# Turning softmax weights: TensorE transposes replaced by 32x32 squares on VectorE and a trip through DRAM

## The chip, the cores and the metric

The kernel runs on one core of a Trainium2 chip. The metric is the device time in microseconds of one execution. Engine names: TensorE is PE in the profile, VectorE is DVE, ScalarE is ACT, GpSimd is POOL, and SyncE (SP) issues most DMAs.

## The reference, cut to what matters

The layer projects x (2048 x 1024) into many columns, runs four branches (stick-breaking attention, pooling, a gated recurrence, attention over a memory), and merges them. The change touches the last one:

```python
def memory_cross_attention(q, mem, w_mem_kv):
    kv = mem @ w_mem_kv
    k = kv[..., :XA_WIDTH].reshape(b, m, XA_HEADS, XA_HEAD_DIM)      # m = 256, 4 heads of 128
    v = kv[..., XA_WIDTH:].reshape(b, m, XA_HEADS, XA_HEAD_DIM)
    scores = jnp.einsum('bshd,bmhd->bhsm', qh, k) / math.sqrt(XA_HEAD_DIM)
    p = jax.nn.softmax(scores, axis=-1)
    out = jnp.einsum('bhsm,bmhd->bshd', p.astype(v.dtype), v)
```

## The kernel before

The sequence is worked in two halves of 1024 rows (T), each in two chunks of 512 (C; c = 0, 1). The projections are 72 "pairs" of 128-column tiles, 36 in each half, each done as 14 "pieces" of six matmuls (a product in three passes, fp32r high and low parts). All engines walk the same list of pieces in an order written out by hand. Work of the branches is hung in between as hooks: on TensorE a hook with number i comes in front of piece i, on the other engines behind their work for piece i. A pair is fed with weights like this: SyncE loads RAW (one half at piece 1, one at piece 12), GpSimd makes sums of them (SR) and, with VectorE, the low parts (WLS, WL), ScalarE the high parts (WHS, WH). ScalarE copies finished banks J out and VectorE adds the others to them (the sums for pieces 5, 9, 11 and 13).

The memory branch takes the pairs XA0 to XA0+3 (queries of head h and its gate), and the first pair of merge 3. In pair XA0+h the weights of head h-1 are finished, and after it the scores of head h are made:

- memory_scores (PE, after the pair): 24 matmuls into BR, c=0 in the banks ZZ, c=1 in AO. Before c=1 it waits for y_f of head h-1, because the values of head h-1 lie in AO.
- memory_max (DVE hook 1), memory_weights (ACT, eight exponentials with row sums into PR), memory_norm (DVE, PR times 1/sum).
- memory_turned: PE turns PR (rows on partitions) into memory positions on partitions, 16 transposes of 128x128 into BR in front of piece 9; ACT hook 8 copies the high part PTH out of PSUM, DVE hook 8 makes the rest PTL = BR - PTH.
- memory_values (PE in front of piece 12): 12 matmuls of VM with PTH and PTL into AO.
- memory_output (DVE hook 12): Y = AO * Y, and y_f rises.
- memory_queries: ACT and DVE hooks 9 and 10 split the queries of head h into XQH and XQL.

There are four heads and two halves, so this runs eight times: six times in a pair XA0+1 to XA0+3, twice in the merge pair, which has no queries and no scores behind it.

Of the kernel before, what the change touches and what calls it, by code (L numbers as in the profile page):

```python
# [39 lines left out]

MEM_TILES = 2 * HEADS

C_ID, C_NEVER, C_CNT = 0, P, 2 * P
# [130 lines left out]
def build(nc, xt, xrow, memt, w8, w4, wgate, wpool, prm, cst, ln_g, ln_b, out):  # L174
    with ExitStack() as ctx:
# [88 lines left out]
        XQR = at("XQR", R + 48, [T])  # L264
        AG = [at(f"AG{i}", R + 52 + 4 * i, [T]) for i in range(2)]
        KM = [at(f"KM{i}", R + 68.25 + i, [MEM], F32R) for i in range(2)]
        VM = [at(f"VM{i}", R + k, [MEM // P, P], F32R) for i, k in enumerate((70.25, 28))]
# [24 lines left out]
        pk_v = nc.dram_tensor("pk_v", (HEADS, P, SEQ // P, 2, P), F32).ap()  # L292
        pk_y = nc.dram_tensor("pk_y", (2, P, T), F32).ap()
        pk_m = nc.dram_tensor("pk_m", (FT, P, T), F32).ap()
        km_keep = nc.dram_tensor("km_keep", (2, P, HEADS * MEM), F32).ap()
# [49 lines left out]
        sc_done, pt_hi, mx_done, ex_done = sem("sc_done"), sem("pt_hi"), sem("mx_done"), sem("ex_done")  # L345
        nm_done, tr_done, pt_done, xo_done = sem("nm_done"), sem("tr_done"), sem("pt_done"), sem("xo_done")

# [49 lines left out]
        def unit(half, u):  # L397

            return raw_block(*PLAIN[u]) if u in PLAIN else sum_of(half, u), XBH[u][:], XBL[u][:]

        def row_number(t, part):
# [25 lines left out]
        def _(sp):  # L427
# [167 lines left out]
            def load_memory_values(half, h):  # L595
# [5 lines left out]
                for i in range(2):  # L601
                    sp.dma_start(VM[i][:].rearrange("p m d -> p (m d)").bitcast(F32),
                                 vm_keep[i, :, h * MEM:(h + 1) * MEM]).then_inc(vm_back, 16)

            def merge(half, n):
                g0 = half * PAIRS + (M0, M1, M2, M3)[n]
# [10 lines left out]
                if n:  # L617
                    def first_weights():
                        if n == 1:
                            sp.wait_ge(mix_done, HEADS * (half + 1))  # L620
                        elif n == 2:
                            sp.wait_ge(xc_f, HEADS * (half + 1))
                        else:
                            sp.wait_ge(sc_done, 4 * HEADS * (half + 1))
                        load_b(half, n, 0)
                    hooks = {8: first_weights}
                    if n == 2:
                        hooks[5] = lambda: order_gates(half, HEADS - 1)
                    pair(g0, hooks)
# [79 lines left out]
            for half in range(HALVES):  # L709
# [15 lines left out]
                for n, first in enumerate((POOL0, LRU0, XA0)):  # L725
                    for h in range(HEADS):
                        hooks = {}
                        if n == 1:
                            hooks = {5: lambda: (load_gate_weights(half, h), h and order_gates(half, h - 1))}
                        if n == 2 and not h:  # L730
                            hooks = {5: lambda: load_memory_values(half, h)}
                        elif n == 2:
                            hooks = {0: lambda: load_memory_keys(half, h), 13: lambda: load_memory_values(half, h)}
                        pair(g0 + first + h, hooks)
                    merge(half, n + 1)
# [35 lines left out]
        def _(pe):  # L771
# [215 lines left out]
            def memory_scores(half, h):  # L987
                hh = half * HEADS + h
                pe.wait_ge(km_back, 32 * (hh + 1))
                pe.wait_ge(xq_lo, hh + 1)  # L990
                if h == 0:
                    pe.wait_ge(mu_done, f_count(half, 2))
                wait_if(pe, pt_done, 4 * hh)
                for c in range(NC):
                    if c:
                        wait_if(pe, y_f, y_count(half, 3, h))
                    for t in range(C // P):
                        q = slice(c * C + t * P, c * C + (t + 1) * P)
                        to = BR[c][t // 2][:, (t % 2) * MEM:(t % 2 + 1) * MEM]
                        mm = pass3(to, (XQH[:, q], XQL[:, q]), (KM[0][:], KM[1][:]), True)  # L1000
                        if t % 2:
                            mm.then_inc(sc_done, 1)

            def memory_turned(half, h):
                hh = half * HEADS + h
                for c in range(NC):
                    pe.wait_ge(nm_done, 4 * (NC * hh + c + 1))
                    for m in range(MEM // P):
                        for t in range(C // P):
                            mm = nc.tensor.transpose(BR[c][m][:, t * P:(t + 1) * P], PR[c][:, t, m * P:(m + 1) * P],  # L1010
                                                     IDENT[:])
                        mm.then_inc(tr_done, 1)

            def memory_values(half, h):
                hh = half * HEADS + h
                pe.wait_ge(pt_done, 4 * (hh + 1))
                pe.wait_ge(vm_back, 32 * (hh + 1))
                for c in range(NC):
                    for m in range(MEM // P):
                        mm = pass3(BR[1][c][:], (VM[0][:, m, :], VM[1][:, m, :]), (PTH[c][:, m, :], PTL[c][:, m, :]), m == 0)  # L1020
                    mm.then_inc(xo_done, 1)

            for half in range(HALVES):
# [17 lines left out]
                for h in range(HEADS):  # L1041
                    pair(g0 + XA0 + h, {9: lambda: memory_turned(half, h - 1),
                                        12: lambda: memory_values(half, h - 1)} if h else {})
                    memory_scores(half, h)
                merge(half, 3, {9: lambda: memory_turned(half, HEADS - 1), 12: lambda: memory_values(half, HEADS - 1)})

# [51 lines left out]
        def _(act):  # L1099
# [182 lines left out]
            def keys_of(h):  # L1282
                act.wait_ge(mk_done, h + 1)
                nc.scalar.copy(KMA[0][:, h, :], KBANK[h][:, 0:MEM]).then_inc(mk_hi, 1)

# [238 lines left out]
            def memory_weights(half, h):  # L1524
                hh = half * HEADS + h
                wait_if(act, tr_done, 4 * hh)
                for c in range(NC):
                    act.wait_ge(mx_done, 2 * (NC * hh + c) + 2)
                    for t in range(C // P):
# [5 lines left out]
            def memory_turned(half, h):  # L1535
                hh = half * HEADS + h
                wait_if(act, xo_done, NC * hh)
                for c in range(NC):
                    for m in range(MEM // P):
                        act.wait_ge(tr_done, 2 * (NC * hh + c) + m + 1)  # L1540
                        if h == 0 and c:
                            wait_kept(act, half, 2, 6)
                        nc.scalar.copy(PTH[c][:, m, :], BR[c][m][:]).then_inc(pt_hi, 1)

# [3 lines left out]
            for half in range(HALVES):  # L1548
# [42 lines left out]
                for h in range(HEADS):  # L1591
                    hooks = {9: lambda: memory_queries(half, h)}
                    if h:
                        hooks[1] = lambda: memory_weights(half, h - 1)
                        hooks[5] = lambda: memory_silu(half, h - 1)
                        hooks[8] = lambda: memory_turned(half, h - 1)
                    pair(g0 + XA0 + h, hooks)
                merge(half, 3, {1: lambda: memory_weights(half, HEADS - 1), 5: lambda: memory_silu(half, HEADS - 1),
                                8: lambda: memory_turned(half, HEADS - 1)})

# [47 lines left out]
        def _(dve):  # L1649
# [124 lines left out]
            def keys_rest(h):  # L1774
                dve.wait_ge(mk_hi, h + 1)
                V_.tensor_tensor(KMA[1][:, h, :], KBANK[h][:, 0:MEM], KMA[0][:, h, :].bitcast(F32),
                                 ALU.subtract).then_inc(mk_free, 1)

# [293 lines left out]
            def memory_norm(half, h):  # L2072
                hh = half * HEADS + h
                for c in range(NC):
# [3 lines left out]
                    for t in range(C // P):  # L2078
                        V_.tensor_scalar(PR[c][:, t, :], PR[c][:, t, :], SM[:, m + 12 + t:m + 13 + t], None,
                                         ALU.mult).then_inc(nm_done, 1)  # L2080

            def memory_queries(half, h):
# [4 lines left out]
            def memory_turned(half, h):  # L2087
                hh = half * HEADS + h
                wait_if(dve, xo_done, NC * hh)
                for c in range(NC):  # L2090
                    for m in range(MEM // P):
                        dve.wait_ge(pt_hi, 2 * (NC * hh + c) + m + 1)
                        if h == 0 and c:
                            wait_kept(dve, half, 2, 7)
                        V_.tensor_tensor(PTL[c][:, m, :], BR[c][m][:], PTH[c][:, m, :].bitcast(F32), ALU.subtract
                                         ).then_inc(pt_done, 1)

            def memory_output(half, h):
                hh = half * HEADS + h
                for c in range(NC):  # L2100
                    dve.wait_ge(xo_done, NC * hh + c + 1)
                    dve.wait_ge(sil, (half * NB + 3) * KB + h + 1)
                    y = Y[h][:, c * C:(c + 1) * C]
                    V_.tensor_tensor(y, BR[1][c][:], y, ALU.mult).then_inc(y_f, 1)

# [39 lines left out]
            for half in range(HALVES):  # L2145
# [58 lines left out]
                def hooks_of(h):  # L2204

                    return {1: lambda: memory_max(half, h), 5: lambda: memory_norm(half, h),
                            8: lambda: memory_turned(half, h), 11: lambda: silu(half, 3, h, AG[h % 2][:]),
                            12: lambda: memory_output(half, h)}

# [296 lines left out]
```

## Time and profile before

| what | value |
|---|---|
| median of 3 runs | 2308.84 us (2308.07 to 2308.89) |
| span of the profiled execution, first to last instruction | 2306.2 us |
| what is listed of the profiled execution's own time | the span alone |
| PE busy | 2293.5 us (99%) |
| PEld, DVE, ACT, POOL busy | 82%, 61%, 46%, 53% |
| granted TensorE clock | 0.999 of full speed |
| DMA | mean 122 GB/s |

The busy shares are over the whole span. Matmuls are pipelined, so a busy PE row says only that PE has no gap. A timeline row has the start, the length, the engine and the line, and for several instructions of a kind in a row their number.

### The profile page before, as it was taken

How to read it: one execution, taken by the hardware profiler on the slowest of the kernel's cores; microseconds unless marked ns; L12 is line 12 of the kernel's file. 1: busy time of each engine (PE TensorE's matmuls, PEld its weight loads, DVE VectorE, ACT ScalarE, POOL GpSimd, SP SyncE). 2: the span in 40 equal slices, each digit the busy share in tenths (PEclk: the TensorE clock that was granted, in tenths of full speed). 3: DMA queues.
4: the chain of work that ended last, by engine and by line, in shares of the span. 5: the costliest groups of instructions: out<-in, count | busy, mean ns of one | idle time of the engine just before them, and what ended most of it. 6: DMA issues, size and time to landing. Idle time of an engine off the chain costs nothing.

```text
span 2306.2 us, 30158 instructions
## 1 busy us (share of the span) xinstructions
PE 2293.5 (99%) x10952; PEld 1901.2 (82%) x10952; DVE 1405.1 (61%) x1658; ACT 1060.3 (46%) x1643; POOL 1219.1 (53%) x847
## 2 busy tenths in 40 slices
PE   9999999999999999999999999999999999999998
PEld 6888888888878888888888888888888778888887
DVE  7556552763476465468877777723744595465476
ACT  5555542442484255332576676632342683355220
POOL 1666653864456354435476566645763555345341
PEclk9999999999999999999999999999999999999999
DMA  6544422124343312374344544332233334312442
GB/s 233 188 157 157 146 73 96 55 83 137 103 112 124 132 51 77 102 275 144 105 161 139 165 154 132 116 99 71 57 126 130 85 110 141 103 55 86 143 168 82
DMA packets 102898, 281.06 MB, mean 122 GB/s; under 512 B 9952, under 2 KB 31584, under 8 KB 101728
## 3 DMA queue, kind: packets, MB, share of 16 engines
q1 hardware_dynamic: 101024, 273.90, 36.2%
q10 hardware_dynamic: 1728, 5.24, 0.7%
q8 instruction: 88, 1.44, 0.3%
q14 instruction: 58, 0.48, 0.1%
HBM read 207.80 MB, written 62.91 MB: 117 GB/s over the span
## 4 chain that ended last, share of the span: by engine, by line
PE 99%; DMA 1%; DVE 0%; issue 0%; DVEq 0%
PE J L775 21%; PE J L777 21%; PE J L776 21%; PE AO L947 8%; PE ZZ L947 8%; PE AO L777 3%; PE AO L776 3%; PE AO L775 3%; PE ZZ L777 2%; PE ZZ L776 2%; PE ZZ L775 2%; PE AO L901 1%; PE JX L901 1%; PE ZZ L982 1%; PE ZZ L870 1%; PE AO L860 0%
## 5 line engine op out<-in xcount | busy, mean ns | idle before, releaser
L2290 POOL TENSOR_TENSOR WLS<-SR,WHS 128x512 fp32r<-128x512 f32 x264 | 407.8, 1563 | 118.8 <-ACT WHS L1118 110.7
L775 PE MATMUL J<-XBH,WHS 128*128 128x512 f32 x1152 | 453.1, 393 | 0.0
L777 PE MATMUL J<-XBH,WLS 128*128 128x512 f32 x1152 | 449.3, 390 | 0.0
L776 PE MATMUL J<-XBL,WHS 128*128 128x512 f32 x1152 | 448.9, 390 | 0.0
L775 PE MATMUL J<-XBH,WH 128*128 128x512 f32 x864 | 340.0, 394 | 0.2
L777 PE MATMUL J<-XBH,WL 128*128 128x512 f32 x864 | 337.0, 390 | 0.0
L776 PE MATMUL J<-XBL,WH 128*128 128x512 f32 x864 | 336.8, 390 | 0.0
L777 PEld LDWEIGHTS J<-XBH,WLS 128*128 128x128 f32 x1152 | 216.2, 188 | 46.0
L776 PEld LDWEIGHTS J<-XBL,WHS 128*128 128x128 f32 x1152 | 216.5, 188 | 43.4 <-issue 0.2
L775 PEld LDWEIGHTS J<-XBH,WHS 128*128 128x128 f32 x1152 | 216.4, 188 | 43.3 <-DVE XBL L1671 0.2
L1704 DVE TENSOR_TENSOR ST<-J,ST 128x512 f32<-128x512 f32 x160 | 109.6, 686 | 228.9 <-PE J L777 178.6
L2282 POOL TENSOR_TENSOR SR<-RAW 128x512 f32<-128x512 f32 x71 | 105.3, 1483 | 269.0 <-DMA RAW<-w 236.8
L2339 POOL TENSOR_TENSOR REST<-REST,SHARE 128x512 f32<-128x512 f32 (+3 forms) x160 | 165.5, 1037 | 118.2 <-DVE REST L1859 114.8
L2356 POOL TENSOR_TENSOR BL<-BRAW,BH 128x512 fp32r<-128x512 f32 x64 | 89.3, 1400 | 222.8 <-ACT BH L1386 222.6
L775 PEld LDWEIGHTS J<-XBH,WH 128*128 128x128 f32 x864 | 162.3, 188 | 39.3 <-issue 7.3
L777 PEld LDWEIGHTS J<-XBH,WL 128*128 128x128 f32 x864 | 162.2, 188 | 34.7
L776 PEld LDWEIGHTS J<-XBL,WH 128*128 128x128 f32 x864 | 162.3, 188 | 31.8 <-issue 0.2
L1118 ACT CAST WHS<-SR 128x1024 fp32r<-128x1024 f32 x144 | 151.5, 1052 | 77.0 <-POOL SR L2282 75.9
L2282 POOL TENSOR_TENSOR SR<-SR,RAW 128x512 f32<-128x512 f32 x71 | 102.6, 1445 | 113.9 <-PE J L777 111.7
L1200 ACT COPY ST<-J 128x512 f32<-128x512 f32 x160 | 94.0, 589 | 139.7 <-PE J L777 136.7
L1859 DVE TENSOR_TENSOR_SCAN REST<-KEEP,REST,ZZ 128x513 f32<-128x513 f32 x96 | 122.8, 1279 | 25.5 <-ACT SHARE L1328 24.4
L2282 POOL TENSOR_TENSOR SR<-RAW,SR 128x512 f32<-128x512 f32 x71 | 101.0, 1422 | 68.2 <-PE J L777 67.5
(302 smaller groups left out, 4748.9 us busy)
## 6 DMA issues: line engine op xcount, KB each, us to landing
RAW<-w SPq DMA_DIRECT2D x144, 512.0 KB, 3.7
pk_m<-MB SPq DMA_DIRECT2D x56, 512.0 KB, 5.0
MB<-pk_m SPq DMA_DIRECT2D x48, 512.0 KB, 4.1
KC<-pk_k SPq DMA_DIRECT2D x40, 512.0 KB, 5.3
VC<-pk_v SPq DMA_DIRECT2D x40, 512.0 KB, 4.4
BRAW<-w SPq DMA_DIRECT2D x64, 256.0 KB, 5.2
XRAW<-xt SPq DMA_DIRECT2D x8, 1024.0 KB, 12.4
pk_v<-STL SPq DMA_DIRECT2D x16, 512.0 KB, 5.1
```

The lines of the kernel that those rows point to most:

```text
L775: nc.tensor.matmul(to, wh, xh, start=first, stop=True, skip_group_check=True)
L776: nc.tensor.matmul(to, wh, xl, start=False, stop=True, skip_group_check=True)
L777: return nc.tensor.matmul(to, wl, xh, start=False, stop=True, skip_group_check=True)
L947: mm = nc.tensor.matmul(BR[p][c][:], w[p][:, k, :], y[k][:, c * C:(c + 1) * C], start=(k == 0 and m == 0), stop=(k == KB - 1 and m == 2))
L1118: nc.scalar.copy(WHS[:, k, :], SR[:, k, :]).then_inc(w_hi, 1)
L1200: nc.scalar.copy(dest(g)[p][:, c * C:(c + 1) * C], J[(g + bank) % 2][:]).then_inc(cp_done, 1)
L1704: V_.tensor_tensor(d, bank[:], d, ALU.add).then_inc(ad_done, 1)
L1859: V_.tensor_tensor_scan(REST[:, j, 0:n + 1], KEEP[:, gs % 2, 0:n + 1], ZB[gs % 2][:, 0:1].broadcast_to([P, n + 1]), 1.0 if diag else REST[ ...
L2282: G_.tensor_tensor(SR[:, 4 * j:4 * j + 4], a, b, op).then_inc(s_raw, 1)
L2290: low = G_.tensor_tensor(WLS[:, k, :], SR[:, k, :], WHS[:, k, :].bitcast(F32), ALU.subtract)
L2339: G_.tensor_tensor(w, w, SHARE[gs % 2][:, 0:n], ALU.mult).then_inc(w_done, 1)
L2356: G_.tensor_tensor(BL[f % 2][:], BRAW[f % 2][:], BH[f % 2][:].bitcast(F32), ALU.subtract).then_inc(b_lo, 1)
```

## The change

The 16 transposes on TensorE go. In their place:

1. The memory keys are stored with their 256 columns in another order, so that the columns of the scores come in four groups (by_group).
2. After the norm of each c VectorE turns PR (128x1024) in one instruction: every 32x32 square is turned in itself, into PB.
3. SyncE (move_blocks, hook 3) writes PB to DRAM, one DMA of 512 KB for each c, and when that has landed reads it back into PR with four DMAs of 128 KB, each to 32 partitions in runs of 1 KB. Now memory positions lie on the partitions.
4. ScalarE copies PTH from PR and VectorE makes PTL from PR and PTH, one 128x1024 instruction for each c instead of two of 128x512 out of PSUM.
5. The hooks move: ACT's exponentials from 1 to 0 and its copies from 8 to 10; DVE's norm from 5 to 3, its silu from 11 to 5, its rests from 8 to 9, its output from 12 to 13; PE's values from 12 to 13, with a wait for each c.

```diff
+        PB = [at(f"PB{c}", R + 4 + 4 * c, [C // P * MEM]) for c in range(NC)]
+        PB_LAST = [at(f"PBL{c}", R + k, [C // P * MEM]) for c, k in enumerate((32, 52))]
+            def move_blocks(half, h):
+                hh = half * HEADS + h
+                for c in range(NC):
+                    sp.wait_ge(pb_made, NC * hh + c + 1)
+                    sp.dma_start(pk_t[c], blocks_of(h)[c][:]).then_inc(pb_kept[c], 16)
+                for c in range(NC):
+                    sp.wait_ge(pb_kept[c], 16 * (hh + 1))
+                    rows = pk_t[c].rearrange("(i r) (g x) -> g r i x", i=GROUPS, g=GROUPS)
+                    for g in range(GROUPS):
+                        to = PR[c][SQUARE * g:SQUARE * (g + 1)].rearrange("p t m -> p (t m)")
+                        sp.dma_start(to.rearrange("p (i x) -> p i x", i=GROUPS), rows[g]).then_inc(pt_in[c], 16)
...
+                    if n == 3:
+                        hooks[3] = lambda: move_blocks(half, HEADS - 1)
...
-                            hooks = {0: lambda: load_memory_keys(half, h), 13: lambda: load_memory_values(half, h)}
+                            hooks = {0: lambda: load_memory_keys(half, h), 3: lambda: move_blocks(half, h - 1),
+                                     13: lambda: load_memory_values(half, h)}
...
-                wait_if(pe, pt_done, 4 * hh)
+                wait_if(pe, ex_done, 4 * NC * hh)
...
-            def memory_turned(half, h):
-                hh = half * HEADS + h
-                for c in range(NC):
-                    pe.wait_ge(nm_done, 4 * (NC * hh + c + 1))
-                    for m in range(MEM // P):
-                        for t in range(C // P):
-                            mm = nc.tensor.transpose(BR[c][m][:, t * P:(t + 1) * P], PR[c][:, t, m * P:(m + 1) * P],
-                                                     IDENT[:])
-                        mm.then_inc(tr_done, 1)
...
-                pe.wait_ge(pt_done, 4 * (hh + 1))
                 pe.wait_ge(vm_back, 32 * (hh + 1))
                 for c in range(NC):
+                    pe.wait_ge(pt_done, NC * hh + c + 1)
...
-                    pair(g0 + XA0 + h, {9: lambda: memory_turned(half, h - 1),
-                                        12: lambda: memory_values(half, h - 1)} if h else {})
+                    pair(g0 + XA0 + h, {13: lambda: memory_values(half, h - 1)} if h else {})
                     memory_scores(half, h)
-                merge(half, 3, {9: lambda: memory_turned(half, HEADS - 1), 12: lambda: memory_values(half, HEADS - 1)})
+                merge(half, 3, {13: lambda: memory_values(half, HEADS - 1)})
...
-                nc.scalar.copy(KMA[0][:, h, :], KBANK[h][:, 0:MEM]).then_inc(mk_hi, 1)
+                nc.scalar.copy(by_group(KMA[0][:, h, :]), by_tile(KBANK[h][:, 0:MEM])).then_inc(mk_hi, 1)
...
-                wait_if(act, tr_done, 4 * hh)
                 for c in range(NC):
+                    wait_if(act, pt_done, NC * (hh - 1) + c + 1)
...
-                    for m in range(MEM // P):
-                        act.wait_ge(tr_done, 2 * (NC * hh + c) + m + 1)
-                        if h == 0 and c:
-                            wait_kept(act, half, 2, 6)
-                        nc.scalar.copy(PTH[c][:, m, :], BR[c][m][:]).then_inc(pt_hi, 1)
+                    act.wait_ge(pt_in[c], 16 * GROUPS * (hh + 1))
+                    if h == 0 and c:
+                        wait_kept(act, half, 2, 6)
+                    nc.scalar.copy(as_product(PTH[c]), as_moved(c)).then_inc(pt_hi, 1)
...
-                        hooks[1] = lambda: memory_weights(half, h - 1)
+                        hooks[0] = lambda: memory_weights(half, h - 1)
                         hooks[5] = lambda: memory_silu(half, h - 1)
-                        hooks[8] = lambda: memory_turned(half, h - 1)
+                        hooks[10] = lambda: memory_turned(half, h - 1)
...
+                    dve.wait_ge(nm_done, 4 * (NC * hh + c + 1))
+                    wait_if(dve, pb_kept[c], 16 * hh)
+                    V_.transpose(blocks_of(h)[c].rearrange("p (g t x) -> p t g x", g=GROUPS, t=C // P), PR[c][:]
+                                 ).then_inc(pb_made, 1)
...
-                        V_.tensor_tensor(PTL[c][:, m, :], BR[c][m][:], PTH[c][:, m, :].bitcast(F32), ALU.subtract
-                                         ).then_inc(pt_done, 1)
+                    V_.tensor_tensor(as_product(PTL[c]), as_moved(c), as_product(PTH[c]).bitcast(F32), ALU.subtract
+                                     ).then_inc(pt_done, 1)
...
-                    y = Y[h][:, c * C:(c + 1) * C]
-                    V_.tensor_tensor(y, BR[1][c][:], y, ALU.mult).then_inc(y_f, 1)
+                    y = Y[h][:, c * C:(c + 1) * C].rearrange("p (t i q) -> p i t q", i=GROUPS, q=SQUARE)
+                    made = BR[1][c].rearrange("p (i t q) -> p i t q", i=GROUPS, q=SQUARE)
+                    V_.tensor_tensor(y, made, y, ALU.mult).then_inc(y_f, 1)
...
-                    return {1: lambda: memory_max(half, h), 5: lambda: memory_norm(half, h),
-                            8: lambda: memory_turned(half, h), 11: lambda: silu(half, 3, h, AG[h % 2][:]),
-                            12: lambda: memory_output(half, h)}
+                    return {1: lambda: memory_max(half, h), 3: lambda: memory_norm(half, h),
+                            5: lambda: silu(half, 3, h, AG[h % 2][:]), 9: lambda: memory_turned(half, h),
+                            13: lambda: memory_output(half, h)}
```

## Rows read from the trace of the kernel before

**Rows 1.** The page: the chain that ended last, shares of the span by engine.
```profile
PE 99%; DMA 1%; DVE 0%; issue 0%; DVEq 0%
```

**Rows 2.** Critical chain, 868 to 895: start us, us, what.
```profile
880.55 0.88 PE ZZ L1010 x8
881.43 0.87 PE AO L1010 x8
```

**Rows 3.** Timeline of PE: start us, us, line, operation, out<-in.
```profile
868.12 0.40 PE L775 MATMUL J<-XBH,WH 128*128 128x512 f32 x1
...
883.29 0.39 PE L777 MATMUL J<-XBH,WLS 128*128 128x512 f32 x1
...
891.48 0.39 PE L777 MATMUL J<-XBH,WL 128*128 128x512 f32 x1
891.71 0.28 PE L775 MATMUL ZZ<-KM,XQH 128*128 128x256 f32 x1
...
893.14 0.28 PE L775 MATMUL AO<-KM,XQH 128*128 128x256 f32 x1
...
894.58 0.40 PE L775 MATMUL J<-XBH,WH 128*128 128x512 f32 x1
```

**Rows 4.** Timeline of DVE, same pair.
```profile
878.58 2.19 DVE L2079 TENSOR_SCALAR PR<-PR,SM 128x256 f32<-128x256 f32 x4
880.69 1.21 DVE L1722 TENSOR_TENSOR WL<-RAW,WH 128x1024 fp32r<-128x1024 f32 x1
...
884.22 0.68 DVE L1704 TENSOR_TENSOR XQR<-J,XQR 128x512 f32<-128x512 f32 x1
...
889.96 1.29 DVE L2104 TENSOR_TENSOR Y<-AO,Y 128x512 f32<-128x512 f32 x2
891.90 0.69 DVE L1704 TENSOR_TENSOR AG<-J,AG 128x512 f32<-128x512 f32 x1 [0.66 <-PE J L777]
```

**Rows 5.** Timeline of ACT, same pair and the one behind it.
```profile
871.60 0.48 ACT L1531 ACTIVATE PR<-ZZ,SM 128x256 f32<-128x256 f32 x1
...
875.21 0.64 ACT L1200 COPY AG<-J 128x512 f32<-128x512 f32 x1
...
884.93 1.06 ACT L1522 ACTIVATE XQH<-XQR 128x1024 fp32r<-128x1024 f32 x1 [0.85 <-DVE XQR L1704]
...
925.29 3.89 ACT L1402 CAST YH<-Y 128x1024 fp32r<-128x1024 f32 x4
```

**Rows 6.** Timeline of POOL, same pair.
```profile
883.82 1.29 POOL L2282 TENSOR_TENSOR SR<-RAW,SR 128x512 f32<-128x512 f32 x1 [3.21 <-PE J L777]
885.25 3.52 POOL L2290 TENSOR_TENSOR WLS<-SR,WHS 128x512 fp32r<-128x512 f32 x2
888.74 2.28 POOL L2282 TENSOR_TENSOR SR<-RAW,RAW 128x512 f32<-128x512 f32 x1
```

**Rows 7.** Timeline of DVE and POOL, 298 to 310.
```profile
301.98 2.32 DVE L1722 TENSOR_TENSOR WL<-RAW,WH 128x1024 fp32r<-128x1024 f32 x1
...
303.18 2.29 POOL L2282 TENSOR_TENSOR SR<-RAW,RAW 128x512 f32<-128x512 f32 x1
...
308.14 0.17 DVE L1832 TENSOR_SCALAR SM<-SM 128x4 f32<-128x4 f32 x1
...
308.19 1.29 POOL L2356 TENSOR_TENSOR BL<-BRAW,BH 128x512 fp32r<-128x512 f32 x1 [2.72 <-ACT BH L1386]
308.35 1.15 DVE L1831 TENSOR_TENSOR SM<-SM 128x4 f32<-128x4 f32 x1
```

**Rows 8.** DMA issues: out<-in, KB each, median us from issue to landing.
```profile
pk_q<-ST SPq DMA_DIRECT2D x8, 512.0 KB, 2.7
...
LI<-XC SPq DMA_DIRECT2D x8, 256.0 KB, 4.6
KM<-km_keep SPq DMA_DIRECT2D x16, 128.0 KB, 2.7
```

**Rows 9.** Timeline of SP's queue, same pair.
```profile
868.31 0.79 SPq L593 DMA_DIRECT2D KM<-km_keep  x2
```

More of the change, by code:

```diff
@@ L41 @@
 MEM_TILES = 2 * HEADS
+SQUARE = 32
+GROUPS = P // SQUARE
 C_ID, C_NEVER, C_CNT = 0, P, 2 * P
@@ L293, in build @@
         pk_y = nc.dram_tensor("pk_y", (2, P, T), F32).ap()
+        pk_t = nc.dram_tensor("pk_t", (NC, P, C // P * MEM), F32).ap()
         pk_m = nc.dram_tensor("pk_m", (FT, P, T), F32).ap()
@@ L345, in build @@
         sc_done, pt_hi, mx_done, ex_done = sem("sc_done"), sem("pt_hi"), sem("mx_done"), sem("ex_done")
-        nm_done, tr_done, pt_done, xo_done = sem("nm_done"), sem("tr_done"), sem("pt_done"), sem("xo_done")
+        nm_done, pt_done, xo_done = sem("nm_done"), sem("pt_done"), sem("xo_done")
+        pb_made, pb_kept, pt_in = sem("pb_made"), [sem(f"pb_kept{c}") for c in range(NC)], [sem(f"pt_in{c}") for c in range(NC)]
         wo_hi = sem("wo_hi")
@@ L399, in unit, with blocks_of, by_group, by_tile @@
             return raw_block(*PLAIN[u]) if u in PLAIN else sum_of(half, u), XBH[u][:], XBL[u][:]
+        def blocks_of(h):
+            return PB_LAST if h + 1 == HEADS else PB
+        def by_group(keys):
+            return keys.rearrange("p (g b r) -> p b g r", g=GROUPS, b=MEM // P)
+        def by_tile(keys):
+            return keys.rearrange("p (b g r) -> p b g r", g=GROUPS, b=MEM // P)
+        def as_moved(c):
+            return PR[c][:].rearrange("p t m -> p (t m)").rearrange("p (n b q) -> p n b q", b=MEM // P, q=SQUARE)
+        def as_product(tile):
+            return tile[:].rearrange("p b (n q) -> p n b q", q=SQUARE)
         def row_number(t, part):
@@ L1593, in _ @@
                     if h:
-                        hooks[1] = lambda: memory_weights(half, h - 1)
+                        hooks[0] = lambda: memory_weights(half, h - 1)
                         hooks[5] = lambda: memory_silu(half, h - 1)
-                        hooks[8] = lambda: memory_turned(half, h - 1)
+                        hooks[10] = lambda: memory_turned(half, h - 1)
                     pair(g0 + XA0 + h, hooks)
-                merge(half, 3, {1: lambda: memory_weights(half, HEADS - 1), 5: lambda: memory_silu(half, HEADS - 1),
-                                8: lambda: memory_turned(half, HEADS - 1)})
+                merge(half, 3, {0: lambda: memory_weights(half, HEADS - 1), 5: lambda: memory_silu(half, HEADS - 1),
+                                10: lambda: memory_turned(half, HEADS - 1)})
                 def split_rows(t, ks):
@@ L1775, in keys_rest @@
                 dve.wait_ge(mk_hi, h + 1)
-                V_.tensor_tensor(KMA[1][:, h, :], KBANK[h][:, 0:MEM], KMA[0][:, h, :].bitcast(F32),
-                                 ALU.subtract).then_inc(mk_free, 1)
+                V_.tensor_tensor(by_group(KMA[1][:, h, :]), by_tile(KBANK[h][:, 0:MEM]),
+                                 by_group(KMA[0][:, h, :].bitcast(F32)), ALU.subtract).then_inc(mk_free, 1)
             def first_sums(second):
@@ L2090, in memory_turned @@
                 for c in range(NC):
[L2091 to L2094, printed above, removed]
-                        V_.tensor_tensor(PTL[c][:, m, :], BR[c][m][:], PTH[c][:, m, :].bitcast(F32), ALU.subtract
-                                         ).then_inc(pt_done, 1)
+                    dve.wait_ge(pt_hi, NC * hh + c + 1)
+                    if h == 0 and c:
+                        wait_kept(dve, half, 2, 7)
+                    V_.tensor_tensor(as_product(PTL[c]), as_moved(c), as_product(PTH[c]).bitcast(F32), ALU.subtract
+                                     ).then_inc(pt_done, 1)
             def memory_output(half, h):
```

## The prediction

> **What bounds the kernel now.** I read the page's chain of waits first: 99% of it is TensorE [rows 1]. No other engine is waited for, so a microsecond comes off the time only if TensorE gets less work, and is lost as soon as TensorE waits. Next I read the timelines of one memory pair on each engine. I count t from the pair's first matmul at 868.12; the next pair starts at 894.58, so a pair takes 26.46 us, without a gap [rows 3]. The reader should see in it: a piece is six matmuls of 0.227 us, 1.36 us; the 16 transposes stand before piece 9; the 24 score matmuls come at the end, the ZZ half (c=0) first and the AO half (c=1) 1.43 us later [rows 3]. In that stretch VectorE, ScalarE and GpSimd idle for much of it, but in short gaps, and what matters is where each step of the softmax lands.
>
> **What is removed.** The 16 transposes of a head: 0.88 + 0.87 us [rows 2]. Eight heads (four in each half), so 8 x 1.75 = -14.0 us, all on the path. The ScalarE and VectorE passes out of PSUM are replaced by passes of the same element count.
>
> **What is free.** The regrouping of the key columns at the start and the permuted views of Y touch the same elements; I cost them at 0 (VectorE's and ScalarE's 1024 elements stay 1024). The scores' wait moves from the rests to the exponentials, long past in both. Dropping the PSUM banks earlier gives nothing, because no one waits for them.
>
> **The new chain, step by step** (pairs XA0+1 to XA0+3, h-1 = 0, 1, 2).
> Maxima: if VectorE is kept by the outputs at the end of the pair before (below), they end at t = 1.3 (c=0) and 2.5 (c=1). Exponentials, at hook 0 now: eight from 871.60 to 875.21, 0.45 each [rows 5], so 1.35 to 3.2 and to 5.0. The piece copy behind them on ScalarE comes at 5.0 instead of 3.0, and TensorE needs it at piece 6, t = 8.2: covered by 3 us.
> Norm: 1.15 us for c=0; for c=1 2.19 us, one of its four having stood while GpSimd ran [rows 4].
> VectorE transposes of 128x1024: the trace has none. Bounds: 0.68 us for 512 elements doubled in rate at the low end, 2.19 us at the high end; nearest is a 1024-element pass, 1.21 us [rows 4]. I take 1.2. Blocks made at t = 5.9 (c=0) and 9.4 (c=1). VectorE's sum after piece 5 slips by 1 us, covered until the next use of that bank.
> SyncE: a 512 KB write lands in 2.7 us (the pk_q row), a 128 KB load in 2.7 us, and an issue takes 0.4 us [rows 8, 9]. SyncE issues c=0's four reads only behind c=1's write (it waits for c=1's blocks first): 9.85 to 11.4, landed by 14.3. The write for c=1 lands at 13, its reads by 17.5. Upper bound for the last of four queued loads is the 4.6 us of LI<-XC [rows 8], which gives 16.0 and 19. What is queued behind these waits on SyncE is the load of RAW at piece 12, which waits for GpSimd's fourth sum, t = 22.9 today [rows 6], and in the merge pair the loads of BRAW, which are split only after that pair: both covered.
> ScalarE, hook 10: it comes behind the cast of the queries, which waits for the sum after piece 9. The sum starts 0.42 us after piece 13's last matmul (891.48, 891.90) and the cast 0.71 after the sum [rows 3 to 5]. Without the transposes piece 9's last matmul starts at 883.29 - 1.75, t = 13.4, so sum 13.85, cast 14.6, and the two copies (0.96 apart, 3.89 us for four [rows 5]) end at 16.6 and 17.6, if c=0 has landed by 15.6.
> VectorE: the rest PTL. Before, one operand lay in PSUM. Now both lie in SBUF, as in WL<-RAW,WH, and that is where I think the cost is.
>
> **Two operands in SBUF beside GpSimd.** A four-element VectorE operation took 1.15 us (its like before it 0.17), from 308.35 to 309.50, while GpSimd ran from 308.19 to 309.48; WL took 2.32 us instead of 1.21, and GpSimd's next one 2.29 instead of 1.29 [rows 4, 7]. So the two take turns: each waits until the other's instruction is over, and whoever waits goes next. The Trainium skill states such a rule (SBUF — State Buffer, "SBUF: two separate sides"): VectorE with two SBUF inputs and GpSimd hold one port pair exclusively. The trace agrees (the 1.15 us).
> Today GpSimd runs SR at 883.82 and two WLS from 885.25 [rows 6]. They follow piece 9, so they move 1.75 earlier: WLS at t = 15.4 to 16.65 and 16.65 to 17.9, then the fourth SR. PTL for c=0 asks at 16.65, when the second WLS starts. I take GpSimd as first (any delay in front of ScalarE's copy gives that, and VectorE's silu, now at hook 5, and its WL, one GpSimd turn apart from t = 10.5 to 13.9, leave the sum after piece 9 no slack): PTL c=0 runs 17.8 to 18.95, SR 18.9 to 20.05, PTL c=1 20.05 to 21.2.
> TensorE reaches the values at 13 x 1.36 = 17.7. It waits to 18.95 (1.25), runs six matmuls to 20.3, waits to 21.2 (0.9). Six times (three pairs in each half): 6 x 2.15 = +12.9 us.
> Behind PTL on VectorE stand the rest of the queries (1.2 us, to 22.4; the scores start at 23.9) and the sum for piece 11, and behind ScalarE's copies its copy for piece 11, which TensorE needs in the next pair: all covered. So is the reload of VM, which waits for the last values and is wanted a pair later.
> In the merge pair there is no query cast; PTL c=0 is ready in time and c=1, behind its load and one GpSimd turn, at 20.0 against 19.05: 2 x 1.0 = +2.0 us.
>
> **The output's new place.** It moves from hook 12 to 13, behind the sum for piece 13, while the AO half of the scores overwrites its bank. The sum starts at 891.90 and takes 0.69, the two outputs take 1.29 [rows 4]: 893.88. The AO scores start at 893.14 [rows 3]: a wait of 0.7 us, six times (after the merge pair no scores follow): +4.2 us. This one I regard as certain; before, the outputs ran at 889.96, inside piece 13.
>
> **Sum.** -14.0 + 12.9 + 2.0 + 4.2 = +5.1 us. The profiled execution spans 2306.2; the median is 2308.84, 2.6 us more for what lies around the span. I add the difference to the median: 2313.9, called 2314.
>
> **Rivals.**
> A, VectorE wins the turn at 16.65: PTL c=0 ends at 17.8, GpSimd's WLS until 18.9, PTL c=1 ends at 20.05. TensorE waits 0.1 and 0.9: 6 x 1.0 = 6.0. Sum -14.0 + 6.0 + 2.0 + 4.2 = -1.8: 2307.0. The two requests are within 0.1 us of each other; for it speaks that ScalarE's copy is reckoned without delay, against it that every delay lies on this side.
> B, the other sign: the rests meet no turn of GpSimd. PTL ends at 17.8 and 18.9, TensorE waits 0.1, and nothing in the merge pair: -14.0 + 0.6 + 4.2 = -9.2: 2299.6. It decides if the second WLS of GpSimd falls outside 16.6 to 17.8 or if this form doesn't take turns; rows 7 speak against the latter.
> C, the loads are late: each read goes to 32 partitions in 1 KB runs, a shape that no row has, and c=1's write runs beside c=0's reads. If c=0 lands at 17 and c=1 at 20.5, PTL c=1 ends at 22.8 (copy 1.05, rest 1.2) instead of 21.2, and in the merge pair at 22.8 instead of 20.0: 6 x 1.6 + 2 x 2.8 = 15 more: 2329; half of that lateness gives 2321. It costs from a landing of c=1 at about 18.9 on. 
>
> **Chances.** Forecast 0.43, A 0.22, B 0.15, C 0.20. 0.2% is 4.6 us, about what a measurement of this kernel can tell from no change. The forecast lies just beyond it: of its 0.43 I put 0.28 on slower and 0.15 on same. A gives same 0.18, faster 0.04. B is faster, C slower. Together faster 0.19, same 0.33, slower 0.48. The forecast's own range is 2310 to 2318 (3 us on each side: half a turn of GpSimd, 0.6 us, in six pairs). The range for 8 in 10 leaves out most of B and the far half of C: 2302 to 2325.
>
> **What the profile after would show.** TensorE's pair from first matmul to first matmul: 27.6 us if I am right (26.46 - 1.75 + 2.15 + 0.7), 26.4 in A, 25.5 in B. TensorE idle before AO<-PTH, put down to PTL, twice in a pair, and idle before AO<-KM put down to VectorE's Y. PTL at about 2.3 us instead of 1.2. The transpose near 1.2 us. In C ScalarE's copy PTH idles for the DMA. Wrong would make it above all a different order of requests near t = 16.6, and a load that lands after 15.6.

## The result, and the profile after

The changed kernel takes 2313.66 us (median of 10 runs, 2313.03 to 2314.68) against 2308.57 us before. The ratio of the two is 1.0023, with a 95% interval of 1.0015 to 1.0032: 5.1 us slower. One of the ten executions of the kernel before took 4679.57 us, for a reason that nothing here shows; without it its median is 2308.56. The profiled execution spans 2311.7 us, 5.5 more than before.

The page of the changed kernel: busy time and instructions, then the chain that ended last by engine.

```profile
span 2311.7 us, 29983 instructions
...
PE 2285.3 (99%) x10824; PEld 1886.3 (82%) x10824; DVE 1444.2 (62%) x1658; ACT 1059.8 (46%) x1627; POOL 1226.4 (53%) x847
...
PE 95%; DVE 2%; DMA 1%; issue 1%; ACT 1%; SPq 0%; DVEq 0%; ACTq 0%
```

TensorE has less work (2285.3 us busy instead of 2293.5), yet it is now 95% of the chain where it was 99% [rows 1]: 4% more of the chain runs through VectorE, ScalarE and issue.

The timeline of TensorE in the pair XA0+3 of the first half. Count t from 869.50, as the prediction counts it from 868.12.

```profile
869.50 0.40 PE L817 MATMUL J<-XBH,WH 128*128 128x512 f32 x1
...
886.98 0.39 PE L819 MATMUL J<-XBH,WL 128*128 128x512 f32 x1
888.61 0.47 PE L817 MATMUL AO<-PTH,VM 128*128 128x512 f32 x1 [1.25 <-DVE PTL L2128]
...
889.85 0.39 PE L819 MATMUL AO<-PTH,VM 128*128 128x512 f32 x1
890.74 0.50 PE L817 MATMUL AO<-PTH,VM 128*128 128x512 f32 x1 [0.50 <-DVE PTL L2128]
...
894.95 0.28 PE L819 MATMUL ZZ<-KM,XQL 128*128 128x256 f32 x1
895.78 0.39 PE L817 MATMUL AO<-KM,XQH 128*128 128x256 f32 x1 [0.55 <-DVE Y L2138]
...
897.32 0.40 PE L817 MATMUL J<-XBH,WH 128*128 128x512 f32 x1
```

The pair takes 27.82 us (869.50 to 897.32) where it took 26.46 [rows 3]. Piece 12's last matmul is at 886.98; the values should follow 0.23 later and come 1.63 later, on PTL. Their second half waits again (889.85 to 890.74), and the AO half of the scores waits for VectorE's Y (894.95 to 895.78, where the next such matmul follows 0.12 later). The three releasers in the brackets are the three that the prediction named.

VectorE in the same pair:

```profile
874.20 1.25 DVE L2113 STREAM_TRANSPOSE PB<-PR 128x1024 f32<-128x1024 f32 x1
...
875.54 1.95 DVE L2109 TENSOR_SCALAR PR<-PR,SM 128x256 f32<-128x256 f32 x4
877.52 1.25 DVE L2113 STREAM_TRANSPOSE PB<-PR 128x1024 f32<-128x1024 f32 x1
...
886.17 4.52 DVE L2128 TENSOR_TENSOR PTL<-PR,PTH 128x1024 fp32r<-128x1024 f32 x2 [2.14 <-ACT PTH L1573]
...
894.44 1.28 DVE L2138 TENSOR_TENSOR Y<-AO,Y 128x512 f32<-128x512 f32 x2
895.64 1.73 DVE L1765 TENSOR_TENSOR WL<-RAW,WH 128x512 fp32r<-128x512 f32 x1
```

The transposes of 128x1024 take 1.25 us. The second norm is 1.95 us with GpSimd in the way [rows 4]. The two rests PTL take 4.52 us together. ScalarE and GpSimd in the same pair:

```profile
885.04 1.03 ACT L1573 CAST PTH<-PR 128x1024 fp32r<-128x1024 f32 x1
886.43 1.05 ACT L1573 CAST PTH<-PR 128x1024 fp32r<-128x1024 f32 x1 [0.36 <-DMA PR<-pk_t]
```

```profile
884.84 2.54 POOL L2324 TENSOR_TENSOR WLS<-SR,WHS 128x512 fp32r<-128x512 f32 x2
887.35 2.26 POOL L2316 TENSOR_TENSOR SR<-RAW,RAW 128x512 f32<-128x512 f32 x1
```

ScalarE's copy for c=0 is done at 886.07 and VectorE asks at 886.17, t = 16.67. GpSimd's first WLS began at 884.84, and the second one starts at 886.10 (its row shows the two as one). VectorE is 0.07 us behind it and waits the whole of it. Then it runs, GpSimd's SR (887.35, 2.26 us instead of 1.29) waits for it, and VectorE's second rest waits for SR in turn.

The pair XA0+1 of the first half, from 815.03, shows the other order. VectorE, then GpSimd:

```profile
831.64 3.45 DVE L2128 TENSOR_TENSOR PTL<-PR,PTH 128x1024 fp32r<-128x1024 f32 x2 [2.07 <-ACT PTH L1573]
835.01 2.30 DVE L2118 SCALAR_TENSOR_TENSOR XQL<-XQR,XQH 128x1024 fp32r<-128x1024 f32 x1
```

```profile
830.39 3.61 POOL L2324 TENSOR_TENSOR WLS<-SR,WHS 128x512 fp32r<-128x512 f32 x2
833.97 2.26 POOL L2316 TENSOR_TENSOR SR<-RAW,RAW 128x512 f32<-128x512 f32 x1
```

Here VectorE asks at 831.64, t = 16.61, 6 ns ahead of GpSimd's second WLS, and goes first: 3.45 us for both rests instead of 4.52, and the pair takes 26.68 us (815.03 to 841.71) instead of 27.8. It is the only one of six in this execution.

All 16 rests, with their shortest, median and longest time in ns, and what TensorE waited for them:

```profile
L2128 DVE TENSOR_TENSOR PTL<-PR,PTH x16: 1226/2296/2322, 831.6 to 2110.8; 128x1024 fp32r<-128x1024 f32 x16
...
  PE AO L817: 10.4, 13
  PEld AO L817: 7.5, 8
```

The new loads, with the median time from issue to landing:

```profile
PR<-pk_t SPq DMA_DIRECT2D x64, 128.0 KB, 3.4
...
```

### The profile page after: what moved, and what is told of

The parts are those of the page before. It is cut to its first block, busy times and chain, and to the rows that moved or that the text cites. A ratio compares the mean times of both kernels' runs of the same rounds, so it can differ in the third digit from the quotient of the medians.

```text
span 2311.7 us, 29983 instructions
## 1 busy us (share of the span) xinstructions
PE 2285.3 (99%) x10824; PEld 1886.3 (82%) x10824; DVE 1444.2 (62%) x1658; ACT 1059.8 (46%) x1627; POOL 1226.4 (53%) x847
## 4 chain that ended last, share of the span: by engine, by line
PE 95%; DVE 2%; DMA 1%; issue 1%; ACT 1%; SPq 0%; DVEq 0%; ACTq 0%
PE J L817 20%; PE J L819 20%; PE J L818 20%; PE AO L989 8%; PE ZZ L989 8%; PE AO L817 2%; PE AO L819 2%; PE AO L818 2%; PE ZZ L819 2%; PE ZZ L818 2%; PE ZZ L817 2%; PE AO L943 1%; PE JX L943 1%; DVE PTL L2128 1%; PE ZZ L1024 1%
```

## The experiments

Every kernel was timed against the kernel before on its own chip. "Difference" is from that kernel's median (2308.46 us in the first four, 2308.18 in the last three); the changed kernel has +5.1.

### The output back at 12

```diff
-                            13: lambda: memory_output(half, h)}
+                            12: lambda: memory_output(half, h)}
```

> The changed kernel with one hook put back: VectorE's outputs of the memory branch at 12 again, ahead of the sum for piece 13. Theory of the output's place: the AO scores wait 0.7 us for Y in six pairs, so that wait goes and the time falls by six times 0.7, 4.3 us, to about 2309.4, and a pair takes 27.1 us instead of 27.8. Rival, the sum for piece 13 is what the next pair needs and only the place of the wait moves: no change, 2313.7.

Measured: 2307.57 us, ratio 0.9995 (0.9986 to 1.0004), a difference of -0.9, so 6.0 us better than the change. TensorE's timeline in the same pair:

```profile
869.11 0.40 PE L817 MATMUL J<-XBH,WH 128*128 128x512 f32 x1
...
888.25 0.47 PE L817 MATMUL AO<-PTH,VM 128*128 128x512 f32 x1 [1.26 <-DVE PTL L2128]
...
890.37 0.50 PE L817 MATMUL AO<-PTH,VM 128*128 128x512 f32 x1 [0.50 <-DVE PTL L2128]
...
896.14 0.40 PE L817 MATMUL J<-XBH,WH 128*128 128x512 f32 x1
```

The pair takes 27.03 us, 0.8 less, and the waits for PTL stand as they were. Five pairs gain 0.8 each, 4.0 us. Not expected were two things. The maxima of the next pair start 1.3 us earlier: the outputs are made sooner, and the WL between them and the maxima takes 0.69 us, where in the changed kernel it meets GpSimd's WLS and takes 1.73 (895.64). So the moved data land sooner, and the wait in the two merge pairs goes, 2.2 us (21.8 us for each up to the next pair, instead of 22.9). There ScalarE's two copies now stand close together, t = 13.85 from that pair's start at 896.14, where they waited 1.09 and 1.26 us for their loads in the changed kernel:

```profile
909.99 2.22 ACT L1573 CAST PTH<-PR 128x1024 fp32r<-128x1024 f32 x2
```

Against that, the pair XA0+1 of the first half lost its turn (26.99 us instead of 26.68). VectorE, then GpSimd:

```profile
831.75 4.60 DVE L2128 TENSOR_TENSOR PTL<-PR,PTH 128x1024 fp32r<-128x1024 f32 x2 [2.07 <-ACT PTH L1573]
```

```profile
830.49 2.55 POOL L2324 TENSOR_TENSOR WLS<-SR,WHS 128x512 fp32r<-128x512 f32 x2
```

VectorE asks at t = 16.61 as it did in this pair of the changed kernel, but this time 4 ns behind the start of GpSimd's second WLS, and waits it out. 4.0 + 2.2 - 0.3 = 5.9.

### GpSimd held until the rests are made

```diff
                 elif i == 9:
                     sum_raw(g + 1, 2)
...
+                    if XA0 < l <= M3:
+                        pool.wait_ge(pt_done, NC * (half * HEADS + l - XA0))
                     if not quiet(g + 1) and not apart:
                         rest_of_sums(g + 1, False)
```

> The changed kernel with GpSimd held: in the eight pairs in which memory weights are turned, GpSimd waits for both rests PTL before its two WLS for the next pair. Theory of the turns: PTL takes 1.2 us instead of 2.3, TensorE waits about 0.1 us for c=0 and up to 0.4 us for c=1 (its load lands near t = 17), instead of 2.3 us in all: 14.4 us of waiting for the rests in eight pairs becomes at most 4, so the time falls by 10 to 14 us, to 2300 to 2303.5. Rival, the moved data are late and PTL is only the messenger: the waits stay where they are, within 1 us in a pair, and the time stays at 2308 or above. Second rival, GpSimd's weights are then late for the next pair: TensorE waits before piece 2 there, and the time stays or rises.

Measured: 2301.68 us, ratio 0.9972 (0.9961 to 0.9983), a difference of -6.8, 11.9 us better than the change. The rests and TensorE's waits for them, all eight pairs:

```profile
L2128 DVE TENSOR_TENSOR PTL<-PR,PTH x16: 1218/1226/1228, 832.0 to 2098.8; 128x1024 fp32r<-128x1024 f32 x16
...
  PE AO L817: 0.9, 5
```

VectorE and GpSimd in the pair XA0+3 of the first half:

```profile
883.90 2.36 DVE L2128 TENSOR_TENSOR PTL<-PR,PTH 128x1024 fp32r<-128x1024 f32 x2 [2.13 <-ACT PTH L1573]
```

```profile
886.34 3.46 POOL L2324 TENSOR_TENSOR WLS<-SR,WHS 128x512 fp32r<-128x512 f32 x2 [3.89 <-DVE PTL L2128]
```

The two rests take 2.36 us instead of 4.52, and TensorE's waits for them 0.9 us in all instead of 17.9. Late data (the first rival) are not what cost the time in these six pairs. That is seen best in the pair XA0+2 of the first half, ScalarE, then VectorE:

```profile
858.29 1.05 ACT L1573 CAST PTH<-PR 128x1024 fp32r<-128x1024 f32 x1 [0.44 <-DMA PR<-pk_t]
```

```profile
859.38 1.23 DVE L2128 TENSOR_TENSOR PTL<-PR,PTH 128x1024 fp32r<-128x1024 f32 x1 [0.20 <-ACT PTH L1573]
```

Here the load holds ScalarE's copy for c=1 until t = 17.01 (the pair starts at 841.28), as late as the 16.93 of the pair XA0+3 above, yet the rest takes 1.23 us and no matmul waits for it. The edit does also make the loads land sooner, by up to 1.5 us for c=1 (pair XA0+3): GpSimd's later WLS no longer meet VectorE's WL in front of the maxima (0.68 us instead of 1.73), and the maxima of the pairs behind another memory pair start 1.1 us sooner. In the merge pairs, where c=1's load did hold up its rest, that helps to end the wait: 21.8 us up to the next pair instead of 22.9. GpSimd's WLS start at t = 19.1 (886.34 less the pair's start at 867.23) instead of 15.3, and no one in the next pair waits for them (the second rival).

### ScalarE's copy for c=0 ahead of the queries

```diff
-                        hooks[10] = lambda: memory_turned(half, h - 1)
+                        hooks[9] = lambda: (memory_turned(half, h - 1, (0,)), memory_queries(half, h))
+                        hooks[10] = lambda: memory_turned(half, h - 1, (1,))
```

> The changed kernel with ScalarE's copy of PTH for c=0 ahead of the cast of the queries, in the pairs with both. Theory of the turns: PTL c=0 then asks near t = 16.1, before GpSimd's first WLS ends, and gets the turn that it lost by 0.08 us, so TensorE waits only for c=1, about 1 us: the five pairs that took 27.8 take about 26.6, so the time falls by about 6 us, to 2307.5. If the queries were what matters (they come 1 us later), the scores in ZZ would wait and nothing would be gained: 2313 or more. Rival, the loads for c=0 land only near t = 16: gain below 2 us.

Measured: 2305.83 us, ratio 0.9990 (0.9981 to 0.9999), a difference of -2.6, 7.7 us better than the change. ScalarE and VectorE in the pair XA0+3 of the first half, which starts at 867.19:

```profile
882.13 1.05 ACT L1573 CAST PTH<-PR 128x1024 fp32r<-128x1024 f32 x1 [1.00 <-DMA PR<-pk_t]
...
884.38 1.05 ACT L1573 CAST PTH<-PR 128x1024 fp32r<-128x1024 f32 x1 [0.24 <-DMA PR<-pk_t]
```

```profile
883.28 1.64 DVE L2129 TENSOR_TENSOR PTL<-PR,PTH 128x1024 fp32r<-128x1024 f32 x1 [1.55 <-ACT PTH L1573]
885.46 1.69 DVE L2129 TENSOR_TENSOR PTL<-PR,PTH 128x1024 fp32r<-128x1024 f32 x1 [0.54 <-ACT PTH L1573]
```

No engine does less here; VectorE only asks at t = 16.09, while GpSimd's first WLS still runs, and the rests fall to 1.64 and 1.69 us. This pair takes 26.55 us (foretold 26.6), as three others do. The first memory pair of each half takes 25.47: there TensorE waits for no rest at all, which had not been foretold and accounts for the 1.7 us beyond the expected gain. ScalarE's first copy waited for its load until t = 14.94, which tells when c=0 lands: 14.9, and c=1 at t = 17.2 (884.38), against 14.3 and 17.5 foretold. The prediction's estimate from the Trainium skill's rate for 32 partitions (SBUF — State Buffer, "Door 1: The DMA port swizzle") was near 15 and near 18; for c=0 the run agrees with it more closely (14.94), for c=1 it does not (17.2). The rate itself is not measured by this, since SyncE issues the eight loads over 4.36 us, one in 0.5 us or so.

### GpSimd held and the output at 12

Both edits together.

> Both of the first two edits. If the two waits are separate, the gains add: 10 to 14 and 4.3, to 2295.5 to 2299, faster than the kernel before. If one hides the other: no better than the better of the two alone.

Measured: 2296.91 us, ratio 0.9950 (0.9937 to 0.9962), a difference of -11.6. The output's place gives 4.8 us on top of the held GpSimd (-6.8 to -11.6), which is 0.8 in six pairs: the two waits are separate. The merge pair's, which the second edit also cured alone, is already gone by the first; in this execution 0.1 and 0.4 us of it come back. Pairs take 25.1 us.

### The kernel before with only its last hooks moved

```diff
-                                        12: lambda: memory_values(half, h - 1)} if h else {})
+                                        13: lambda: memory_values(half, h - 1)} if h else {})
...
-                            12: lambda: memory_output(half, h)}
+                            13: lambda: memory_output(half, h)}
```

> The kernel before with only the hooks of the values and of the output moved, both from 12 to 13; transposes, PSUM banks and all else as they were. Theory of the output's place: TensorE waits before the AO scores for Y in six pairs and nowhere else, 0.7 to 0.8 us each as after the change: 4.2 to 4.9 us more, 2312.7 to 2313.4. Rival, the wait comes only with the new chain: no change, 2308.5.

Measured: 2312.92 us, ratio 1.0020 (1.0011 to 1.0029), a difference of +4.7. TensorE's timeline in the pair XA0+3:

```profile
870.08 0.40 PE L775 MATMUL J<-XBH,WH 128*128 128x512 f32 x1
...
894.98 0.28 PE L777 MATMUL ZZ<-KM,XQL 128*128 128x256 f32 x1
895.81 0.39 PE L775 MATMUL AO<-KM,XQH 128*128 128x256 f32 x1 [0.55 <-DVE Y L2104]
...
897.35 0.40 PE L775 MATMUL J<-XBH,WH 128*128 128x512 f32 x1
```

The place of the output costs its 4.7 us in the kernel before as well, with transposes and all: six pairs, 0.8 each (27.27 us instead of 26.46). No matmul waits in front of the values, so it is not their move that costs.

### A quarter of the transposes

```diff
-                        for t in range(C // P):
+                        for t in (C // P - 1,):
```

> The kernel before with 4 of a head's 16 transposes, one for each bank, so three quarters of the turned weights are left out of the computation. Each transpose costs TensorE 0.109 us (1.75 for 16), so 12 x 8 of them give 10.5 us: 2298.0. If the transposes lay partly beside other work, less: 2301 or more.

Measured: 2301.05 us, ratio 0.9967 (0.9954 to 0.9979), a difference of -7.1; the span falls by 8.1 (2298.1). That is 2.4 to 3.4 us short of what was expected, and the median lies where the expectation's rival has it (2301 or more, if the transposes lay partly beside other work), so the time alone does not decide between the two. The trace does. TensorE around the four that are left:

```profile
878.27 0.38 PE L1010 MATMUL ZZ<-IDENT,PR 128*128 128x128 f32 x2
878.70 0.44 PE L1010 MATMUL AO<-IDENT,PR 128*128 128x128 f32 x2
878.89 0.48 PE L775 MATMUL J<-XBH,WHS 128*128 128x512 f32 x1
```

From 878.27 to the next piece at 878.89 four transposes take 0.62 us, where four times 0.109 is 0.44: six transposes fewer would bring the AO half 0.65 us sooner after the first, and VectorE's norm for c=1 is not yet done then. The view by tile says so:

```profile
its engine sat idle before it (us, times) until:
  DVE PR L2079: 2.3, 8
```

That is 0.29 us in each of eight pairs. 10.5 - 2.3 = 8.2 us, and the spans differ by 8.1. So the price of a transpose holds, and a new wait took 2.3 us of it back (the last run, without any of the 16, gives 1.80 us for them); the expectation had left out that the norm was only just in time (878.58 + 2.19 = 880.77 [rows 4], with the AO half's first transpose at 881.4 [rows 2]). Why three of the five executions took 1 us more than the profiled one is open.

### All three edits

The changed kernel with GpSimd held, the output at 12 and the copy for c=0 ahead.

> All three edits of the changed kernel: GpSimd held, output at 12, ScalarE's copy for c=0 ahead of the queries' cast. TensorE waits 0.3 to 0.4 us before the values for c=0 in six pairs with the first two; that goes, and up to 0.2 us may come back before c=1, whose load lands near t = 17: 1 to 2 us less than with two, 2295 to 2296.

Measured: 2294.33 us, ratio 0.9939 (0.9927 to 0.9952), a difference of -13.9: better than both kernels, and 0.7 below the expected range. TensorE, first matmul of the pair XA0+3 and first matmul behind it:

```profile
864.91 0.40 PE L817 MATMUL J<-XBH,WH 128*128 128x512 f32 x1
...
889.57 0.40 PE L817 MATMUL J<-XBH,WH 128*128 128x512 f32 x1
```

The pair takes 24.66 us, 1.80 less than before, and TensorE waits for nothing in any of the memory pairs. The gain is the whole of the removed transposes: 1.80 us in six pairs and 1.76 in the two merge pairs (21.79 instead of 23.55), 14.3 us, 13.9 measured. Against the run with two edits a memory pair takes 0.46 us less (25.12 to 24.66), where 0.3 to 0.4 had been expected, and the 0.1 and 0.4 in the merge pairs go too.

## Why the prediction was right

- **The transposes, -14.0.** Measured -14.3: 26.46 to 24.66 us for a pair without waits, six times, and 23.55 to 21.79 for a merge pair, twice.
- **The rests, +12.9.** In the pair above TensorE loses 27.82 - 24.66 = 3.16 us in all; 0.8 of it is the output's (the out-at-12 run), 2.34 the rests'. Five pairs at 2.34 and one at 1.2 make 12.9. The forecast had six at 2.15. The two waits are 1.40 and 0.66 us (foretold 1.25 and 0.9); the other 0.28 is lost behind them, since the matmuls behind a wait follow each other more slowly (0.31 and 0.34 us to the next one in the timeline, against 0.23). One pair went the way of rival A.
- **The turns.** Shown by the hold run: the same rests take 1.23 us with GpSimd held and 2.30 beside it. The Trainium skill's rule (SBUF — State Buffer, "SBUF: two separate sides"), by which the two engines hold one port pair exclusively, agrees with it. That the order is decided by less than 0.1 us was also right: in five of the six pairs VectorE asks 0.06 to 0.07 us behind the start of GpSimd's second WLS and waits, in the sixth it asks 6 ns ahead of it and goes first. Why it asks 0.06 us sooner there no run shows. Rival A is thus not refuted but was dealt one pair of six in the profiled execution; how often it comes in the others was not seen, and their spread of 1.65 us, where one such pair is worth 1.1, says little: the kernel before spreads over 1.26 without that turn.
- **The output's place, +4.2.** Measured +4.7 to 4.9, in the changed kernel and alone in the kernel before. This was called certain and is. The wait is the 0.7 us foretold, and another 0.1 goes to the slow start behind it (895.78 to 896.00 for the first matmul, against 0.12).
- **The merge pair, +2.0.** Measured +2.2: 22.9 us up to the next pair with the wait, 21.8 without it, twice. The four terms make 5.7, the spans differ by 5.5. The second rest there ended at t = 19.97 (20.0 foretold). What the prediction did not see is what this wait hangs on, which is when the maxima begin: with the output at 12 they begin 1.3 us sooner, with GpSimd held and the output still at 13 they begin 1.1 us sooner, and the wait goes either way. Part of that delay is once more a turn, VectorE's WL at 1.73 us instead of 0.69.
- **The chain up to the blocks.** Transpose 1.25 (foretold 1.2), blocks at 5.95 and 9.27 (5.9, 9.4), PTL's request at 16.67 (16.65).
- **Rival B** (no turns, 2299.6) describes what the hold run made of the kernel: 2301.7. **Rival C** (late loads) did not occur; ScalarE waited up to 0.70 us for c=1 in the six pairs, and this cost nothing there, because GpSimd's turn ended later still. What a later landing would cost was not tried.

The difference came out at 5.1 us, as the sum has it, though the terms as measured make 5.7. Part of the agreement is luck: the output's and the transposes' terms were off by 0.7 and 0.3 in opposite directions, and the rests' by a pair that was cheaper and five that were dearer.

## What to carry to other kernels

Work that is moved off the bounding engine takes its operands along: an operand that moves from PSUM to SBUF can make a VectorE instruction wait for GpSimd, so look at what GpSimd runs at that very time, not at how busy it is. (The sum XQR, with one operand in PSUM, took its 0.68 us at 884.22 in the midst of GpSimd's SR at 883.82 [rows 4, 6].) Before giving up such a change, hold the engine in the way with a wait if its work is not due soon; here that turned +5.1 us into -6.8, and to -13.9 with two hooks more. A result that frees a bank for the next work must be taken out before that work's turn comes; one hook later cost 4.7 us by itself.

## What had not been expected of the hardware

That two engines' order could turn on so little: VectorE's request 6 ns ahead of GpSimd's start gave a pair of 26.68 us, 0.06 to 0.07 us behind it gave 27.8, 1.1 us of time; and in the run with the output at 12, 4 ns behind were enough to wait.

And that VectorE's 32x32 transpose of 1024 fp32 elements takes 1.245 to 1.247 us in every one of its runs, with GpSimd at work or not. In the pair XA0+1 of the first half the second one runs beside GpSimd's SR nearly from end to end, and neither is longer than elsewhere:

```profile
820.89 1.25 DVE L2113 STREAM_TRANSPOSE PB<-PR 128x1024 f32<-128x1024 f32 x1
```

```profile
820.80 1.30 POOL L2316 TENSOR_TENSOR SR<-RAW 128x512 f32<-128x512 f32 x1 [3.85 <-DMA RAW<-w]
```

So this form, with one operand, takes no turns with GpSimd here, while the rest PTL, with two operands in SBUF, does.
